# Stick-breaking heads: two score products merged into one of 256 columns, halves added on VectorE; gate's bias one slot later in three of four places

## The reference

```
def stick_breaking_attention(q, k, v):
    ...
        z = jnp.einsum('bhqd,bhsd->bhqs', qc, k).astype(jnp.float32) * scale
        past = s_pos[None, :] < t[:, None]
        log_fail = jnp.where(past, jax.nn.log_sigmoid(-z), 0.0)
        later = lax.cumsum(log_fail, axis=3, reverse=True) - log_fail
        w = jnp.where(past, jnp.exp(jax.nn.log_sigmoid(z) + later), 0.0)
        return jnp.einsum('bhqs,bhsd->bhqd', w.astype(v.dtype), v)
...
    gates = jax.nn.sigmoid(jnp.concatenate([g_a, g_b], axis=-1) + b_gate)
    merged = gate_a * (y_a @ w_branch_moba) + gate_b * (y_b @ w_branch_sb)
    return merged @ w_out
```

## Time and profile before

| | us |
|---|---|
| median of 3 runs | 1114.3 (1114.27 to 1114.58) |
| the profiled execution, its own time | 1114.35 |
| its span in the trace | 1112.5 |
| TensorE busy | 1106.8 |
| VectorE busy | 790.6 |
| ScalarE busy | 621.2 |

### The profile page before, as it was taken

How to read it: one execution, slowest core, us unless ns; L and a number is a source line. 1 busy time by engine, 2 the same in 40 slices (tenths; PEclk the granted TensorE clock), 3 DMA queues, 4 the chain that set the end, 5 groups by cost and what they waited for, 6 DMA issues and landing times.

```text
span 1112.5 us, 14865 instructions
## 1 busy us (share of the span) xinstructions
PE 1106.8 (99%) x5830; PEld 941.2 (85%) x5830; DVE 790.6 (71%) x1136; ACT 621.2 (56%) x825; POOL 58.0 (5%) x105
## 2 busy tenths in 40 slices
PE   9999999999999999999999999999999999999998
PEld 8888888888888888888888888888877788888887
DVE  6777754667987677775477787557898786777752
ACT  6556542677656456554356556337787854656530
POOL 1000000100000000000000000011343000000000
PEclk9999999999999999999999999999999999999999
DMA  9755565654454665555565555557643455555541
GB/s 317 252 190 189 189 246 190 211 162 141 165 195 157 203 189 190 189 189 189 191 206 190 189 189 189 189 154 255 224 150 122 149 181 164 191 188 194 192 179 38
DMA packets 142581, 208.02 MB, mean 187 GB/s; under 512 B 9296, under 2 KB 100584, under 8 KB 142512
## 3 DMA queue, kind: packets, MB, share of 16 engines
q1 hardware_dynamic: 139408, 198.07, 52.7%
q0 software_dynamic: 3088, 9.00, 2.4%
q10 hardware_dynamic: 16, 0.00, 0.0%
HBM read 205.98 MB, written 2.65 MB: 188 GB/s over the span
## 4 chain that ended last, share of the span: by engine, by line
PE 98%; ACT 1%; DMA 0%; issue 0%; DVE 0%; SPq 0%; ACTq 0%; DVEq 0%
PE banks L1810 28%; PE banks L1696 16%; PE banks L1698 16%; PE banks L1697 16%; PE banks L1807 14%; PE banks L1768 1%; PE banks L2046 1%; PE banks L1718 1%; PE banks L1983 1%; DMA raw<-in_ffn_w_gate 0%; PE banks L2076 0%; PE banks L2073 0%; PE banks L2142 0%; PE banks L2016 0%; PE banks L2019 0%
## 5 line engine op out<-in xcount | busy, mean ns | idle before, releaser
L1143 DVE TENSOR_TENSOR w_lo<-raw,w_hi 128x2048 fp32r<-128x2048 f32 x186 | 422.7, 2275 | 167.8 <-ACT w_hi L752 167.5
L752 ACT ACTIVATE w_hi<-raw 128x2048 fp32r<-128x2048 f32 x186 | 352.2, 1897 | 111.8 <-PE banks L1698 108.2
L1810 PE MATMUL banks<-xT,w_hi 128*128 128x512 f32 x1344 | 314.5, 390 | 0.0
L1810 PEld LDWEIGHTS banks<-xT,w_hi 128*128 128x128 f32 x1344 | 249.2, 188 | 49.7
L1696 PE MATMUL banks<-w_hi,xT 128*128 128x512 f32 (+1 forms) x432 | 170.4, 394 | 0.0
L1807 PEld LDWEIGHTS banks<-xT,w_lo 128*128 128x128 f32 x1344 | 167.4, 191 | 3.4
L1807 PE MATMUL banks<-xT,w_lo 128*128 128x256 f32 x1344 | 169.8, 283 | 0.0
L1698 PE MATMUL banks<-w_hi,xT 128*128 128x512 f32 (+1 forms) x432 | 167.0, 387 | 0.0
L1697 PE MATMUL banks<-w_lo,xT 128*128 128x512 f32 (+1 forms) x432 | 166.7, 386 | 0.0
L1696 PE MATMUL banks<-w_hi,hT_hi 128*128 128x512 f32 x352 | 137.3, 390 | 0.0
L830 ACT ACTIVATE gate<-gate 128x256 f32<-128x256 f32 x84 | 35.1, 418 | 182.5 <-DVE gate L1272 182.5
(11 more groups left out here) (324 smaller groups left out, 900.1 us busy)
## 6 DMA issues: line engine op xcount, KB each, us to landing
raw<-in_ffn_w_gate SPq DMA_DIRECT2D x88, 512.0 KB, 3.7
raw<-in_ffn_w_up SPq DMA_DIRECT2D x88, 512.0 KB, 4.7
raw<-in_ffn_w_down SPq DMA_DIRECT2D x88, 512.0 KB, 4.1
raw<-in_w_in SPq DMA_DIRECT2D x76, 512.0 KB, 4.4
raw<-in_w_out SPq DMA_DIRECT2D x16, 512.0 KB, 4.0
raw<-in_w_branch_moba SPq DMA_DIRECT2D x4, 512.0 KB, 4.4
raw<-in_w_branch_sb SPq DMA_DIRECT2D x4, 512.0 KB, 4.9
raw<-in_w_branch_a SPq DMA_DIRECT2D x4, 512.0 KB, 4.2
```

The source lines that it names most:

```text
L752: act.activation(w_hi[u % SLOTS][:, 0:n], raw[u % RAWS][:, 0:n], ACT.Copy).then_inc(hi_done, 1)
L1143: dve.tensor_tensor(w_lo[r][:, 0:n], raw[r][:, 0:n], w_hi[u % SLOTS][:, 0:n], ALU.subtract).then_inc(lo_done, 1)
L1810: m = pe.matmul(bank[b + s], mh, xT[:, k].rearrange("p a s -> p (a s)"), start=first, stop=k == KC - 1, skip_group_check=c == 0)
```

## The change

In the scores of a stick-breaking head, the two 128-column products for key rows 128 to 255 (with m1 and with m2, summed in PSUM) become one product of 256 columns, whose two halves land side by side in columns 256 to 511 of the bank. sb_clamp adds them up: first the second half plus the mask (128 columns, side_added), then the mask to columns 0 to 255, then the first half plus the result of the first add, and the clamp as before. A softmax head waits for side_added by its place in all heads (it.m) now, since stick-breaking heads count there too.

gate_rows is called at q == 1 and not q == 0 for j = 7, 8 and 9 (slots 29, 33, 37), and stays at slot 40 for j = 10.

```diff
--- before.py
+++ after.py
@@ -1452,7 +1452,7 @@
                     bias = {"fox": cum_bias(h), "dsa": soft[h % 2][:], "moba": causal}[kind]
                     dve.tensor_tensor(s[:, 0:P], S[:, SC:NB], bias[:, 0:P], ALU.add).then_inc(side_added, 1)
                     masked(slice(P, SC), bias[:, P:SC], k + 1)
-                    dve.wait_ge(side_added, it.softs + 1)
+                    dve.wait_ge(side_added, it.m + 1)
                     masked(slice(0, P), s[:, 0:P], k).then_inc(read_d, 1)
 
                 def invert(it):
@@ -1474,7 +1474,11 @@
                     else:
                         dve.wait_ge(weighed, it.sbs - 1)
                     s = score[it.m % 2]
-                    dve.tensor_tensor(s[:], bank[4 + it.i % 2][:, 0:SC], past, ALU.add).then_inc(read_d, 1)
+                    S = bank[4 + it.i % 2]
+                    dve.tensor_tensor(s[:, SEQ:SC], S[:, SC:NB], past[:, SEQ:SC], ALU.add).then_inc(side_added, 1)
+                    dve.tensor_tensor(s[:, 0:SEQ], S[:, 0:SEQ], past[:, 0:SEQ], ALU.add)
+                    dve.wait_ge(side_added, it.m + 1)
+                    dve.tensor_tensor(s[:, SEQ:SC], S[:, SEQ:SC], s[:, SEQ:SC], ALU.add).then_inc(read_d, 1)
                     dve.wait_ge(read_d, it.read)
                     dve.tensor_scalar(soft[it.m % 2][:], s[:], 30.0, None, ALU.min).then_inc(clamped, 1)
 
@@ -1611,7 +1615,7 @@
                     for it in ITEMS[b]:
                         if it.kind == "SM" and it.what[0] != "fox" and slot - it.slot == SM_AT["inv"]:
                             invert(it)
-                    if b == 0 and q == 0 and 7 <= j <= 10:
+                    if b == 0 and 7 <= j <= 10 and q == (j < 10):
                         dve.wait_ge(tri_done, 1)
                         gate_rows(j - 1)
                     if b == 1:
@@ -2009,8 +2013,8 @@
                         st, m1, m2, both = operands(it)
                         pe.matmul(S[:, 0:SEQ], st[:, 0:P], m1, start=True, stop=False)
                         pe.matmul(S[:, 0:SEQ], st[:, 0:P], m2, start=False, stop=True)
-                        pe.matmul(S[:, SEQ:SC], st[:, P:SEQ], m1[:, P:SEQ], start=True, stop=False)
-                        pe.matmul(S[:, SEQ:SC], st[:, P:SEQ], m2[:, P:SEQ], start=False, stop=True).then_inc(scored, 1)
+                        pe.matmul(S[:, SEQ:NB].rearrange("p (a c) -> p a c", c=P), st[:, P:SEQ], both[:, :, P:SEQ],
+                                  start=True, stop=True).then_inc(scored, 1)
                     elif it.kind == "SM":
                         st, m1, m2, both = operands(it)
                         pe.matmul(S.rearrange("p (a c) -> p a c", c=P)[:, 0:4:3, :], st[:, 0:P], both[:, :, 0:P],
```

## The result

| | before | after |
|---|---|---|
| median of 18 runs each, us | 1114.28 | 1116.2 |
| lowest to highest, us | 1114.07 to 1114.80 | 1115.66 to 1117.83 |
| the profiled execution, us | 1114.35 | 1115.66 |
| its span, us | 1112.5 | 1113.9 |

The ratio is 1.0021, 95% interval 1.0014 to 1.0027. By the medians the kernel is slower by 1.9 us (0.17%), 0.7 more than the forecast; by the means it is 2.3 us (0.20%). That it is slower is clear; on which side of the 0.2% that the prediction took as no change it lies is not, since the interval holds both sides. Within that, after has two kinds of executions: eleven of the 18 had a mean granted clock of 1.000 (1115.66 to 1116.38, median 1115.87), seven had 0.998 (1117.35 to 1117.83, median 1117.60). The profiled one is of the first kind.

The account below looks back on a forecast made before the run. PE's own stream bounds the kernel: from 1114.35 us, a new wait costs +1.5 after swallowing heads 0 to 4's gain, heads 5 to 7 return 0.3, net +1.2, 1115.5 us. Range 1113.4 to 1116.6.

Parts of the forecast that it names:

- The product on PE: First-block stick-breaking heads: the merged product saves PE 0.11 us a head, 0.9 us over eight heads.
- The rule that the prediction set against it: Skill's cycle table for PE: two 128-column matmuls cost only 6 cycles more than one of 256, 2.5 ns a head.
- rival 4: The merge is worth nothing on PE; the same wait without a gain, +1.5 us, 1115.9; chance 0.03.
- The adds: VectorE, each stick-breaking head: three adds take 0.87 us instead of 0.59, so e, the extra per head, is 0.28 us.
- The biases: VectorE: the 1.32 us pair leaves the gap before head 1's next step and stands behind head 2's clamp.
- How late VectorE becomes: VectorE's queue up to head 4's clamp: 2.11 us late, starting at 304.26 and not 302.15.
- The wait of 2.1: PE at head 3's sum waits 2.1 us for ScalarE's copy of heads 0 and 1; net +1.2 us.
- Heads 5 and 7: Later PE sums on the same chain: about 0.5 us of room stays at head 7, so no wait was counted.
- rival 2: PE's clock falls from 2.4 to 1.2 GHz behind the new wait; 1118.3 for one slot; chance 0.07.
- L = 2.8: Full-clock PE work, in us, slowed to 1.2 GHz behind the wait; it takes 2.8 us longer.
- nothing in the second mixer: After 337 us VectorE's own waits for PE take up its delay, so no later cost was counted.
- Rival 1: No new PE wait, as VectorE and ScalarE find their time elsewhere; only the product counts, 1113.5; chance 0.11.

Follow-up runs that it names:

- the old products' run: After, with the two old 128-column products instead of the merged one and a minimum in place of the last add; 1116.34 us (1.0019).
- version with early copy and unmoved biases: After, with biases at their old slots 28, 32, 36 and ScalarE's copy of heads 0 and 1 ahead of slot 32's weight split; 1113.82 us (0.9997).
- The sixteen copies: Before, with sixteen one-column VectorE copies added at slot 43 of the first mixer; 1114.69 us (1.0004).
- The early copy: After, with ScalarE's copy of heads 0 and 1 moved ahead of slot 32's high part of a weight tile; 1115.09 us (1.0007).
- eight copies: Before, with eight linked 128-column ScalarE copies added ahead of the PSUM copy of heads 0 and 1; 1116.65 us (1.0028).
- twelve copies: Before, with twelve linked 128-column ScalarE copies added ahead of the PSUM copy of heads 0 and 1; 1119.76 us (1.0049).
- thirty-two instructions more: The version with early copy and unmoved biases plus sixteen one-column VectorE copies at slot 43, 32 VectorE instructions more than before; 1113.29 us (0.9993 against before).

## Why the prediction went as it did

**The product on PE** was right: 0.36 us from the merged product to the second large one in after against the 0.35 that was read from a softmax head, 0.12 a head by the old products' run, 0.11 by the version with early copy and unmoved biases. The rule that the prediction set against it, and its rival 4, rest on figures which the Trainium skill (TensorE: Matmul & The Clock Gate, Back-to-back issue gap) gives for a matmul by itself.

**The adds** were right and a little smaller: 0.21 + 0.33 + 0.31 = 0.85 against 0.87, e = 0.26 and not 0.28. The estimate of 0.38 by the Trainium skill (VectorE: DVE Perf Modes, The TRN2 errata) is not borne out.

**The biases** went where the prediction put them, with the gap ahead of head 1's next step empty. That step starts at 289.60; taken from the start-up's 0.24 it was expected at 289.66.

**How late VectorE becomes, and who waits**: head 4's clamp at 303.92 against 304.26, the copy's end at 307.60 against 307.96, PE's start at 307.75 against 308.01. Of these 0.3 us, 0.24 is the start-up and 0.1 the smaller e; PE goes on 0.15 behind the copy's end and not 0.05. The wait of 2.1 was reckoned from the start that the sum would have had; counted so it is 2.1 in after as well (305.43 + 0.23 to 307.75), and 1.93 is the part that the list counts. The net in the first mixer is 1.20 against 1.2.

**Heads 5 and 7** were right in after: no wait at either. The copy before head 7's sum ended 2.33 later than before (328.76 against 326.43) and PE came at 329.73, which is 1.0 of room and not 0.5. ACT and PE, in order of time in after, against the earlier trace rows:

```profile
328.40 0.36 ACT L996 ACTIVATE y_b<-banks 128x256 f32<-128x256 f32 x1
...
329.73 0.33 PE L2062 MATMUL banks<-soft_hi,tri_r 128*128 128x384 f32 x1
```

**What failed** is three things beside the sum.

First, *rival 2, the clock*, with its chance of 0.07. The prediction saw that a wait of 2 us in mid-kernel was new and that the clock could fall behind it, and then put "a granted clock of 1.00 throughout" as what the profile would show. It had only waits up to 1.1 us to read from the earlier trace rows, none of which says anything on 2 us. The forecast and rival 2 are not two outcomes of the kernel: after has both, 11 and 7 of 18 executions, and the seven are 1.7 us longer at their median (1117.60 - 1115.87). The size was put at L = 2.8, and is 1.7. The median of the mixture lies 0.3 above that of the undisturbed part. The Trainium skill (TensorE: Matmul & The Clock Gate, What's actually happening) says that the clock is set by how busy PE has been recently; the rows behind the wait of 2.0 us, where it is 0.50, agree.

Second, *nothing in the second mixer*. The sum stopped at the last place that the diff touches; the 0.35 us at 787 us is a term that it put at nothing. Its only reason was that DVE's later waits take up DVE's delay, which they do; a gap that comes from the number of instructions it did not consider. The sixteen copies show that it comes with the count of instructions alone. Nothing in the profile of before gave its size; what could have been seen there is that DVE goes without a gap from the gates' operations to that low part, with the dk_sides that PE needs behind it, so that anything that delays DVE there ends on PE.

Third, *the list of rivals treated the waits one by one*. Rival 1, no new wait, was given as 1113.5. The early copy took nearly all of the predicted wait away and the time was 1115.09, since 0.3 of it stayed and two others opened, at heads 5 and 7. The way to 1113.5 leads over ACT's lateness as a whole.

Without the first two the sum gives 1114.28 + 1.20 = 1115.5, which is the forecast to the tenth; with the 0.35 it is 1115.8 (1115.87 measured), with the clock 1116.2. So the failed step is that the sum ended with the wait of 2.1 us: it gave that wait no price in the clock and the second block no term, and these two made the missing 0.7. The direction was right, and the time lies in the range. But the prediction gave 0.86 to a change too small to be told from none, and the kernel is slower clear of the noise (1.0014 to 1.0027). Whether it is within 0.2% stays undecided: the border is at 1116.5 by the median, which is 1116.2, and the ratio is 1.0021. Without the clock alone, or without the 0.35 alone, the median would be near 1115.9.

## What to carry to other kernels

Where PE is the bound and an in-order neighbour is the one behind which it will wait, a gain on PE ahead of that wait is worth nothing and only the part behind it counts; so sum the neighbour's lateness first, at every place where PE takes a result from it, and look whether removing the longest wait opens the next. A listed wait of PE cost 0.2 us more than its length here. A new wait of 2 us in a stream that had hardly idled had a second price in the clock here: give it an own term, as a share of executions times its size, not a small chance. And an edit that changes the number of instructions can shift a small gap far behind it into a tight place or out of one, so compare the starts of one repeated operation over the whole span before explaining the total.

## What the runs showed of the hardware that was not expected

- The clock fell from 1.00 to 0.50 (2.4 to 1.2 GHz) behind a single wait: with eight copies only after PE had gone on at full pace (restart at 309.02), with twelve before the restart at 310.09. The mean clock was 0.998 or less in 0 of 11 executions with a wait of 1.0 us, 0 of 11 with 1.2, 1 of 11 with 1.3, 7 of 18 with 1.9, 3 of 7 with 2.0 and 4 of 5 with 3.3. It cost 1.7 us in after (1117.60 against 1115.87), and with twelve copies once 3.2 (1121.34 against 1118.11, mean clock 0.997).
- One execution of the version with early copy and unmoved biases had 0.998, and the trace of another execution of it has no such wait. That is open. PE's wait at 8 us, in the start-up, differs between the profiled executions (up to 1.6 us), so a longer one there is possible and not shown.
- Behind a wait the second matmul starts 0.25 us after the first, and not 0.17. With the 0.16 by which the modelled end of a large product overhangs, PE lost 0.73 for a listed wait of 0.52 and 1.17 for 0.95.
- Sixteen one-column DVE copies at 335 us cost nothing there and 0.35 us at 787 us, 450 us later; thirty-two instructions more and the 0.35 was gone. In all seven traces the gap stands behind DVE's 831st instruction.
